# A two-layer diffusion block: the last scatter goes tile by tile into the closing normalisation, the SiLU of the convolution branch moves into the merge, and a few steps change engine or place

## The reference, cut to what matters

```python
def _conformer_conv(u, w_dw, b_dw, g, b):              # branch C, 512 channels
    a, gate = jnp.split(u, 2, axis=-1)
    y = a * jax.nn.sigmoid(gate)
    y = depthwise_conv(y, w_dw, 31 taps) + b_dw
    return jax.nn.silu(_layer_norm(y, g, b))

def _merge(h, ys, w_branch, w_gate, b_gate, w_out):    # ys = branches A, B, C, D
    g = jax.nn.sigmoid(h @ w_gate + b_gate)
    z = g[..., :D_MODEL] * (ys[0] @ w_branch[0])
    for i in range(1, N_BRANCH):
        z = z + g[..., i * D_MODEL:(i + 1) * D_MODEL] * (ys[i] @ w_branch[i])
    return z @ w_out

# a layer
hl = _layer_norm(xl) * (1.0 + sc1) + sh1
yl = _token_mixing(hl, ...)        # one projection; A windowed GQA, B neighbourhood attention,
                                   # C conformer convolution, D bidirectional mLSTM in chunks of 128; _merge
xl = _layer_norm(alpha * xl + g1 * yl, ln1_g, ln1_b)
hl = _layer_norm(xl) * (1.0 + sc2) + sh2
ml = _expert_choice_ffn(hl, ...)   # 16 experts; y summed back: zeros.at[ib].add(yb)
xl = _layer_norm(alpha * xl + g2 * ml, ln2_g, ln2_b)
```

## Time and profile before

| what | value |
|---|---|
| time, median of 3 runs | 3564.94 us (3562.6 to 3565.64) |
| the profiled execution, its time | 3567.71 us |
| its span, first to last instruction | 3565.9 us |
| mean granted clock of PE | 0.958 |
| busy: PE, DVE, ACT, POOL | 91%, 63%, 49%, 20% of the span |
| D stage of layer 0, layer 1 | 522 to 648 us, 2369 to 2471 us |
| mLSTM stage | 648 to 708 us, 2471 to 2523 us |
| O stage | 708 to 750 us, 2523 to 2551 us |
| merge | 750 to 1163 us, 2551 to 2821 us |
| last scatter and closing | 3535 to 3566 us |

### The profile page before, as it was taken

The page is one execution under the profiler, slowest core; times in us unless marked ns, Lnnn a source line. Parts: engine busy times, 40 slices in busy tenths (PEclk is TensorE's granted clock), DMA queues, the critical chain, the costliest instruction groups (busy, mean ns, idle before and its releaser), DMA issues. The chain is left out here.

```text
span 3565.9 us, 49308 instructions
## 1 busy us (share of the span) xinstructions
PE 3261.8 (91%) x18708; PEld 2750.8 (77%) x18708; DVE 2262.3 (63%) x3362; ACT 1732.9 (49%) x2169; POOL 704.8 (20%) x531
## 2 busy tenths in 40 slices
PE   7999889899999979999999399899899969999996
PEld 4987569799999757777777388578788757777885
DVE  3685871621222539999999584763313448999998
ACT  3112762422122547777776622754222347777775
POOL 3001012323322112222121100013344301111111
PEclk8999999999999979999999699999999979999998
DMA  7265025312221339999999244122233218999996
GB/s 262 79 168 141 5 77 181 93 50 101 84 92 50 137 116 336 334 330 334 337 334 349 76 101 102 33 97 76 86 112 95 96 72 310 350 343 352 362 359 249
DMA packets 445700, 647.09 MB, mean 181 GB/s; under 512 B 131662, under 2 KB 214078, under 8 KB 438622
## 3 DMA queue, kind: packets, MB, share of 16 engines
q1 hardware_dynamic: 304960, 557.88, 45.2%
q0 software_dynamic: 24096, 79.60, 6.8%
q10 hardware_dynamic: 116480, 7.35, 2.2%
HBM read 625.01 MB, written 27.08 MB: 183 GB/s over the span
## 5 line engine op out<-in xcount | busy, mean ns | idle before, releaser
L954 PE MATMUL ps<-hx,part 128*128 128x384 f32 (+2 forms) x5088 | 977.4, 352 | 16.7 <-POOL part L590 5.5
L954 PEld LDWEIGHTS ps<-hx,part 128*128 128x128 f32 x5088 | 883.5, 190 | 104.7 <-issue 16.9
L1416 PE MATMUL ps<-part,hx 128*128 128x512 f32 x3072 | 748.1, 396 | 19.8 <-DVE hx L2487 11.4
L1416 PEld LDWEIGHTS ps<-part,hx 128*128 128x128 f32 x3072 | 573.3, 189 | 152.4 <-issue 12.9
L2470 DVE TENSOR_TENSOR part<-raw,part 128x2048 fp32r<-128x2048 f32 x256 | 600.6, 2347 | 24.1 <-ACT part L1782 23.2
L1782 ACT ACTIVATE part<-raw 128x2048 fp32r<-128x2048 f32 x256 | 490.6, 1917 | 147.1 <-DMA raw<-in_w_exp_up 63.5
L590 POOL TENSOR_TENSOR part<-raw,part 128x2048 fp32r<-128x2048 f32 x66 | 303.8, 4603 | 638.6 <-ACT part L587 638.4
L1416 PE MATMUL ps<-hx 128*128 128x512 f32 x1536 | 379.6, 395 | 3.8 <-DVE hx L2470 1.3
L1416 PEld LDWEIGHTS ps<-hx 128*128 128x128 f32 x1536 | 286.7, 188 | 77.9 <-issue 7.7
L587 ACT ACTIVATE part<-raw 128x2048 fp32r<-128x2048 f32 x100 | 190.6, 1910 | 277.3 <-PE ps L954 159.9
L2470 DVE TENSOR_TENSOR hx<-raw,hx 128x2048 fp32r<-128x2048 f32 x128 | 294.2, 2298 | 31.0 <-ACT hx L1782 29.5
(11 more groups left out here) (314 smaller groups left out, 3679.6 us busy)
## 6 DMA issues: line engine op xcount, KB each, us to landing
raw<-in_w_exp_gate SPq DMA_DIRECT2D x128, 1024.0 KB, 6.0
raw<-in_w_exp_up SPq DMA_DIRECT2D x128, 1024.0 KB, 6.2
raw<-in_w_exp_down SPq DMA_DIRECT2D x128, 1024.0 KB, 6.6
raw<-in_w_mod SPq DMA_DIRECT2D x48, 1024.0 KB, 5.8
raw<-in_w_in SPq DMA_DIRECT2D x44, 1024.0 KB, 5.8
raw<-in_w_gate SPq DMA_DIRECT2D x32, 1024.0 KB, 5.3
raw<-in_w_branch SPq DMA_DIRECT2D x16, 1024.0 KB, 5.1
area<-rows_d POOLq DMA_DIRECT2D x40, 256.0 KB, 4.5
```

Source lines behind the costliest of these rows:

```text
L954: last = mm(dst, a, b, start=i == 0, stop=i == len(pairs) - 1)
L1416: last = mm(ps[:, bank, :], x, y, start=kh == 0 and a == 0, stop=kh == 1 and a == len(pairs) - 1)
```

## The change

- The last scatter (both layers) takes its chunks by tile (`last_order`): both halves of tile 0, then of tile 1, and so on. In the last layer DVE adds the two chunks of a tile, waits for each add, and runs `close_sum` of that tile; the barrier between scatter and closing is gone for all four engines. The wait for `rows2` and `x1` stands after the first tile's adds. In the last layer POOL stores the tiles before its only barrier there.
- `conv_silu(j)` leaves the end of the D stage. ACT runs it in the merge at `it` = 0, behind the sigmoid of gate group j. The wait for `conv_normed` goes, since a barrier lies between.
- `turn_rows` and `conv_sum` change places between PE's groups; on ACT `copy_rows` moves from 6 to 7 and `conv_root` from 14 to 13.
- The low part of block S_O + 1 moves from POOL, end of the mLSTM stage, to DVE, start of the O stage. POOL waits for it at the start of its list for the O stage.
- In the last iteration of the merge `z_low(4)` to `z_low(6)` follow `z_low(1)` to `z_low(3)` instead of standing after the loop.

```diff
+def last_order(per):
+    return sorted(range(per), key=lambda c: (scattered(c)[1], scattered(c)[0]))
...
@@ POOL, mLSTM and O stages
-                split.mixers_to(l, S_O + 2)
-                st.leave()
-
+                st.leave()
+
+                split.mixers_from(l, S_O + 2)
                 load(ys[:, FB * TOK:2 * FB * TOK], yb_d).then_inc(*S("parked", l).by(16))
@@ POOL, end
-                st.leave()
-
-                if l == DEPTH - 1:
+                if l < DEPTH - 1:
+                    st.leave()
+                else:
                     for t in range(full):
                         pool.wait_ge(*S("x2", l).at(NT + t + 1))
                         load(out[0, t * P:(t + 1) * P, :], x2v[:, t, :]).then_inc(*S("x_out", l).by(16))
@@ PE, D stage
-                        {1: gate_sums, 2: turn_inputs, 3: turn_maxima, 5: turn_rows, 6: conv_sum, 12: conv_squares},
+                        {1: gate_sums, 2: turn_inputs, 3: turn_maxima, 5: conv_sum, 6: turn_rows, 12: conv_squares},
@@ PE, last scatter
-                for c in range(per):
-                    pe.wait_ge(*S("e_acc", l).at(E // 2 * per + 1 + max(c - 3, 0)))
-                    scatter(c, c % 4, slice(0, P) if c < 2 * TL else slice(0, CAPC))
-                st.leave()
-
-                if l == DEPTH - 1:
-                    st.leave()
+                for k, c in enumerate(last_order(per)):
+                    pe.wait_ge(*S("e_acc", l).at(E // 2 * per + 1 + max(k - 3, 0)))
+                    scatter(c, k % 4, slice(0, P) if c < 2 * TL else slice(0, CAPC))
+                st.leave()
@@ ACT, D stage
                 def conv_silu(j):
-                    act.wait_ge(*S("conv_normed", l).at(j + 1))
                     fn(y_v[2][:, j, 0:nt], y_v[2][:, j, 0:nt], ACT.Silu, bias=conv_c[:, j, KS + 2:KS + 3],
                        scale=conv_c[:, j, KS + 1:KS + 2])
...
-                       {4: gate_exps, 6: copy_rows, 7: lambda: (conv_square(0), conv_square(1)), 8: lambda: conv_square(2), 9: lambda: conv_square(3),
-                        14: conv_root})
-                for j in range(FB):
-                    conv_silu(j)
+                       {4: gate_exps, 7: lambda: (copy_rows(), conv_square(0), conv_square(1)), 8: lambda: conv_square(2),
+                        9: lambda: conv_square(3), 13: conv_root})
                 st.leave()
@@ ACT, merge
                         last.then_inc(*S("z_gate", l).by(1))
+                        if it == 0:
+                            conv_silu(j)
@@ DVE, end of the D stage
-                    V.tensor_tensor(y_v[2][:, j, 0:nt], y_v[2][:, j, 0:nt], cstd[:, 0:nt], ALU.mult
-                                    ).then_inc(*S("conv_normed", l).by(1))
+                    V.tensor_tensor(y_v[2][:, j, 0:nt], y_v[2][:, j, 0:nt], cstd[:, 0:nt], ALU.mult)
@@ DVE, O stage
+                split.mixers_from(l, S_O + 1)
+                split.mixers_to(l, S_O + 2)
                 for g in range(2 * full):
@@ DVE, merge
                             if it == 2 * NBR - 1:
                                 z_low(j)
+                                if j:
+                                    z_low(FB + j - 1)
...
-                for k in range(FB, KD - 1):
-                    z_low(k)
                 st.leave()
@@ DVE, last scatter and closing
-                for c in range(per):
-                    add(c, c % 4, E // 2 * per)
-                st.leave()
-
+                order = last_order(per)
+                for k in range(per if ctx_out else 0):
+                    add(order[k], k % 4, E // 2 * per, k)
                 if l == DEPTH - 1:
-                    dve.wait_ge(*S("rows2_in", l).at(48))
-                    dve.wait_ge(*S("x1_in", l).at(16 * full))
                     for t in range(full + 1):
                         if t < full:
+                            for k in (2 * t, 2 * t + 1):
+                                add(order[k], k % 4, E // 2 * per, k)
+                                dve.wait_ge(*S("e_acc", l).at(E // 2 * per + 1 + k + 1))
+                            if t == 0:
+                                dve.wait_ge(*S("rows2_in", l).at(48))
+                                dve.wait_ge(*S("x1_in", l).at(16 * full))
                             close_sum(t, NT)
                         if t:
                             close_norm(t - 1, NT).then_inc(*S("x2", l).by(1))
-                    st.leave()
+                st.leave()
```

More of the change, by code:

```diff
@@ L154 @@
 o_turned z_part z_sum z_hi z_lo ym_hi ym_lo p_y xn xn_hi h2_tmp xn_T left_in aff_out picked r_logits r_aff r_affT r_slotT g_out g_mm e_acc e_hid e_turned e_hH e_hL
-e_yH e_yL e_comb var std conv_sig conv_cent conv_var conv_std conv_normed m_abs m_log m_exps m_gate
+e_yH e_yL e_comb var std conv_sig conv_cent conv_var conv_std m_abs m_log m_exps m_gate
 p_var p_std z_gate r_cent r_exp e_sil q_mu q_std v_std v_nb xhat_n conv_part ab_part d_part ab_out d_out
@@ L2471, in rest, with add @@
                                     ).then_inc(S("split_v"), 1)
-                def add(c, bank, base):
-                    dve.wait_ge(*S("e_comb", l).at(base + (c + 2)))
+                def add(c, bank, base, nth=None):
+                    dve.wait_ge(*S("e_comb", l).at(base + ((c if nth is None else nth) + 2)))
                     half, t = scattered(c)
```

## The result

The changed kernel takes 3544.19 us (median of 5 runs, 3540.18 to 3548.33) against 3565.64 us for the kernel before (5 runs, 3562.6 to 3574.8): ratio 0.9934, 95% interval 0.9919 to 0.995. The forecast was 3543 (3536 to 3554). The medians are 21.4 us apart. The profiled execution spans 3542.5 us where it spanned 3565.9: 23.4 us less.

What follows compares the result with a forecast made beforehand. PE was taken to set the time in the mixer stages, with barrier drains setting stage starts and DVE alone at the end. Terms summed to -22.2 us, from the 3564.94 median to 3542.8, forecast 3543, range 3536 to 3554.

Steps and rivals of the forecast that it cites:

- Step 1: D stage ends: removing table load and SiLUs saves 5.1 us (layer 0), 4.2 (layer 1); higher clock afterwards 1.5.
- Step 2: D stage, layer 0: swapping turn_rows and conv_sum saves 4.4 us, 3.02 of wait plus a group's 10.04 - 8.60.
- the root: D stage: conv_root one group earlier is a table load and one pass under PE's groups, worth 0.
- Step 3: mLSTM end: without POOL's split the mask ends 3.82 us sooner, 7.6 over two layers; clock 1.0 more.
- Step 4: Merge's first step: SiLUs and table loads on ACT nearly fit the 3.5 us margin; cost 0.3, bounds 0 and 3.
- Step 5: Merge's tail, layer 0: two of DVE's four low parts move up, saving 1.35 us; layer 1 0.
- Step 6: Last layer's closing: adds waiting for themselves and a stall for x1 cost 2.7 us, bounds 0.7 and 3.5.
- clock terms: PE's higher clock gains 1.5 us at layer 1's mLSTM start and 1.0 in the last mLSTM products of both layers.
- given back: Rival, chance 0.18: swap, clock and merge's tail give nothing, merge's first step costs 1 to 3; about 3553 us.
- no change: Rival, chance 0.06: something else sets the stages' starts and SiLUs and mask merely cover it; 3560 to 3567 us.
- slower through ACT: Rival, chance 0.04: ACT's price per merge channel block exceeds the 3.5 us margin, so PE waits; 3579 us at price 8.

Runs made afterwards that it cites:

- e2: The changed kernel with the four SiLUs put back at the end of the D stage: 3555.07 us, ratio to the kernel before 0.9965.
- e4: The changed kernel with the split of block S_O + 1 on POOL instead of DVE, at the O stage's start: 3547.22 us, ratio to before 0.9936.
- e7: The changed kernel with turn_rows and conv_sum back in their old places and copy_rows one group earlier: 3543.66 us (one run).
- e10: The changed kernel with all eight last-layer adds before the closings, plus unused PE matmuls in waits at the mLSTM and merge ends: 3538.88 us, ratio to before 0.9897.

## Why the prediction was right, step by step

- **Step 1, SiLU out of the D tails.** Predicted 5.1 and 4.2; undoing it costs 5.06 and 4.21. Right. The clock of 1.00 behind it in layer 1 came too; it was put at 1.5 and is worth 1.7 (e2 against e4). In layer 0 0.4 is given back behind it, at a wait for ACT that the sum didn't have (e2).
- **Step 2, the swap.** Predicted 4.4. The D stage of layer 0 is shorter by 9.84 in all, less 5.06 for step 1: 4.8. Of this the order is worth 3.24 by itself (e7). The other 1.5 is the size of the slow group's loss, which the term counted with the order's (1.44); it is the clock's and is not bound to the wait. It leaves next to nothing for the root, as predicted.
- **Step 3, the mask.** PE's wait fell from 6.07 to 2.25, 3.82 a layer, as predicted; DVE's split is hidden. Place, not engine (e4).
- **Step 4, the merge's first step.** Predicted +0.3 with bounds 0 to 3; it is 0, but the working came out by luck. ACT's price of a block is 2 x 1.28 + 0.81 = 3.4 in layer 1, near the 3.3 taken. The term set one block's price against the margin of 3.5, though, and two blocks, 6.7 us, stand ahead of the low part that PE needs. It came only 2.63 nearer to PE, since ACT had idle time that the term left out (2.95 us before its second sigmoid). The next activation starts 0.02 us after a load. By the 2.66 us a switch that the Trainium skill gives (ScalarE: Activation LUTs, "What ACT_TABLE_LOAD costs") the margin would have been passed, as the prediction estimated; these rows don't show its drain, and the measurement decides.
- **Step 5, the merge's tail.** Predicted 1.35, shown 1.53.
- **Step 6, the closing.** Predicted +2.7 with bounds 0.7 and 3.5. Measured +3.2 up to DVE's last operation, as x1 came 0.6 us later than estimated, and +4.0 with POOL's longer drain, a term that the sum didn't have. The direction and both causes, the stall and the adds in pairs, held.
- **The clock.** This is the step that failed, though it hardly shows in the total. A higher clock gave 1.7 at the mLSTM end of layer 0 (eight pairs of products, each issued 0.22 and not 0.43 us behind the one before), 0.6 at that of layer 1 (the same eight in 3.15 and not 3.78 us), 1.50 in the O stage of layer 0, 1.57 at the start of its merge, 1.7 at the mLSTM start of layer 1 and the 1.5 of step 2: 8.6 us. A lower one took 2.40 and 2.58 in attention and O stage of layer 1 (over the attention 0.94 granted, 0.96 before) and 1.02 and 1.08 in the two output projections: 7.1, at the same work. That nets 1.5 us of gain, where the prediction had 1.5 + 1.0 and the 1.44 in step 2: 3.9. It named places where the clock would rise, and none where it would fall.

The sum of the parts themselves, -5.06 - 4.21 - 3.24 - 7.64 - 1.53 + 4.0 = -17.7 us, is close to what the prediction gave them without its clock terms (-18.3, with 3.02 for step 2). The trace shows -23.4. Of the other 5.7 the clock's balance is 1.5, less the 0.4 given back behind step 1, and 4.6 lies in stages whose work the diff leaves alone but for the order of layer 0's last scatter (the front and the experts of both layers, the routing of layer 0), which adds up to within 0.1 us; the experts of layer 0 alone took 635.7 to 643.2 us over the twelve kernels. Why those stages differ was not tried. So the total agrees in part by luck: the clock gave 2.4 us less than counted, the closing cost 1.3 more, and 4.6 us from stages that hardly belong to the change made it up. Of the rivals, "given back" as it was priced (9 to 11 us) and "no change" are excluded by the stages' rows; "slower through ACT" was 0.87 us away.

## What to carry to other kernels

Cost each part of a change in its own stage, by what ends last there; parts of one change can have both signs, and here the one in the title was the loss. When a barrier is removed to overlap two steps on one engine, ask whether that engine has any idle time to fill: DVE had 0.8 us of idle time in a stretch of 26.5, so the new order only moved a wait for a load ahead of work that used to cover it. What is gained at one barrier can be lost at the next: here the last drain grew by more than the barrier had cost. A function put into a stage that seems to have room is free up to a margin that can be read from the trace, and that has to be read again afterwards.

## What was not expected

- The same instructions behind the same wait came at either clock: the group behind turn_rows in 10.04 or 8.57 us, 48 products in 6.01 or 8.59, the O stage of layer 1 in 27.9, 29.4 or 30.5 us. The Trainium skill, TensorE: Matmul & The Clock Gate, "Part 1: The HAM clock gate", says that how many of one kernel's first matmuls are slow varies from run to run with the phase of the chip's activity monitor at its start. Here low stretches come and go in the middle of a kernel; the merge's start in e10 and in the changed kernel would fit a phase, but no run here varies the phase alone.
- Behind waits of 2.25 us at the mLSTM ends of the changed kernel the clock fell in layer 1 and stayed in layer 0.
- POOL's last drain takes 1.11 us in every kernel with the new closing and 0.37 before.
- Eight switches of ACT's table in a layer, 10.3 us of loads, moved no end of a stage.
